# The second feed-forward product by seven block products instead of eight, with the splits of its tokens in another order

## Chip, cores and metric

One core of a Trainium2 chip. The metric is the device time of one execution in microseconds; the kernel before was run three times. The profiled execution is a run of its own.

## The reference, cut to what matters

Two transformer blocks in a row on 1024 tokens of width 1024, float32. The change touches the last lines of the second block, above all the second product:

```python
def second_block(x, c, ..., w_ff1, w_ff2):
    ...
    x = x + g1 * _hybrid_mixer(h, w_in[l], ...)
    h = _rms(x, norm2_w[l]) * (1 + sc2) + sh2
    x = x + g2 * (jnp.square(jax.nn.relu(h @ w_ff1[l])) @ w_ff2[l])
    return x
```

`w_ff1` is 1024 x 4096, `w_ff2` 4096 x 1024. Every product of the kernel keeps float32 accuracy with three matmuls: each operand is split in a high part (rounded to the type that TensorE multiplies) and a low part (the rest), and high x high, high x low and low x high are added in PSUM.

## The kernel before, in words

The kernel is one program of some fifteen stages, each written once per engine in fixed order, with semaphores between the engines. Weights lie in `wts` as slabs of 128 x 1024 numbers; activations lie transposed, features on the 128 partitions, tokens along the row, in two halves of 512 tokens.

**First product.** `mixer_out_stage` makes the first quarter of the 4096 hidden features in full (eight tiles x two halves). `ffn_stage` makes the other three quarters in 12 pairs of tiles. A pair is a 2 x 2 block product (two halves of the depth, two halves of the tokens, two tiles of features) done by the Winograd form of Strassen's scheme: seven products (`PRODUCTS`, line 2309) on four weight blocks and the sums S1 to S4 of them, against four token blocks and combinations of these that `mixer_out_stage` prepared. One product is 12 matmuls of 128 x 512 (four depth steps x three), a pair 84. GpSimd makes S1 to S4 and the seven low parts (lines 3660 to 3668), ScalarE the seven high parts (`pair_high`, line 3199) and a copy of the first product (line 3574), VectorE adds up the results out of six banks (`add`, line 3591), takes the square of the positive part (`square`, line 3599), and ScalarE's queue stores the four result blocks of 256 KB to `fd` in HBM (`store`, line 3552). SyncE's queue loads a pair's weights, three transfers of 1 MB together (lines 3691 to 3695), released by a product of the pair two before.

**Second product.** It is a plain product. The 4096 hidden features are taken in eight eighths of four tiles. For each eighth SyncE loads its tokens from `fd` in one transfer of 2 MB (`f_load`, line 3702), ScalarE makes four high parts of 1024 numbers a row (`eighth_high`, line 3563), VectorE four low parts (`eighth_low`, line 3604). Weights come as 512 KB for two output tiles through a ring of three (`ring_load`, line 3710); GpSimd casts them and makes the low parts (lines 3676 to 3679). TensorE makes, for each eighth, eight output tiles x two token halves, 12 matmuls each, in two banks by turns:

```python
for e in range(EIGHTHS):
    for f in range(KT):
        ...
        for c in range(2):
            pe.wait_ge(s_x2, 2 * i + c + 1)
            for j in range(KH):
                ...
```

VectorE multiplies each result by the gate and adds it to `x2` in SBUF (line 3644, one update for 12 matmuls); behind the last eighth SyncE stores each output tile of 512 KB (line 3739). In the last pair of the first product the two parts overlap: the first ring and token loads, the first eighth's splits on ScalarE (line 3581) and VectorE (lines 3621 and 3626), and the load of `x2`.

**Around it.** `gated_out_stage` closes each branch of the mixer; with `opens` it clears semaphores that later stages take again (lines 2282 to 2284, `k.again`). `leaves` marks the branch of the pooled features, its last use.

## Time and profile before

| | us |
|---|---|
| median of three runs (3139.1 to 3140.5) | 3140.2 |
| the profiled execution | 3137.1 |
| its span, from the first to the last instruction | 3135.3 |
| TensorE matmul busy | 3064.3 (98%) |
| VectorE busy | 1685.8 (54%) |
| GpSimd busy | 1444.7 (46%) |
| ScalarE busy | 987.1 (31%) |

The mean granted clock of TensorE is 0.996 of full speed. Busy time is the time in which an engine has an instruction under way. Matmuls of TensorE are pipelined and their recorded times overlap, so its count of instructions and the distance of their starts say more than the busy time. The span is 1.8 us shorter than the execution.

### The profile page before, as it was taken

Reading aid. Unit: us, or ns where it says so; the run is one execution under the profiler, and the core shown is the slowest. Engines: PE = TensorE matmul, PEld = TensorE weight load, DVE = VectorE, ACT = ScalarE, POOL = GpSimd, SP = SyncE. Lnnn points to the kernel's source line nnn. Section 1 sums busy time; section 2 is a strip of 40 time slices with the busy share of each in tenths; the row PEclk is TensorE's granted clock in tenths of the full one; section 3 lists DMA queues with packets and bytes.
Section 4 is the critical chain, followed back from the end, with each engine's and each line's share of the span. In section 5 each row is a group of like instructions: output and inputs, shape, how many; then the busy total and the mean of one; then the engine's idle time right before and its main releaser. Section 6 shows DMA issues by size and latency. Waiting matters only on the chain.

```text
span 3135.3 us, 39395 instructions
## 1 busy us (share of the span) xinstructions
PE 3064.3 (98%) x15012; PEld 2511.6 (80%) x15012; DVE 1685.8 (54%) x2636; ACT 987.1 (31%) x1520; POOL 1444.7 (46%) x1180
## 2 busy tenths in 40 slices
PE   8999999999999999999999999999999999999999
PEld 5777888887877777778788888888788878878887
DVE  5874666666444786655644343465624554444443
ACT  4445444454312532500433332431211232210000
POOL 3442211211356522223877777545336687743332
PEclk9999999999999999999999999999999999999999
DMA  4321100110144321255122222272124433342222
GB/s 143 101 77 41 34 28 27 34 34 27 48 134 148 95 82 45 70 167 204 49 78 70 65 64 83 81 221 71 49 88 161 144 118 116 116 178 101 101 102 87
DMA packets 119661, 288.84 MB, mean 92 GB/s; under 512 B 9904, under 2 KB 36144, under 8 KB 118080
## 3 DMA queue, kind: packets, MB, share of 16 engines
q1 hardware_dynamic: 75984, 219.25, 21.8%
q10 hardware_dynamic: 43504, 67.19, 6.2%
q8 instruction: 120, 1.97, 0.3%
q14 instruction: 53, 0.43, 0.0%
HBM read 239.05 MB, written 47.35 MB: 91 GB/s over the span
## 4 chain that ended last, share of the span: by engine, by line
PE 90%; DVE 6%; ACT 1%; issue 1%; DMA 1%; DVEq 0%; POOL 0%; ACTq 0%; SPq 0%; PEldq 0%; PEld 0%; POOLq 0%
PE proj_bank L236 13%; PE proj_bank L238 13%; PE proj_bank L237 13%; PE proj_bank L2492 4%; PE proj_bank L2494 4%; PE proj_bank L2493 4%; PE proj_bank L3544 4%; PE proj_bank L3546 4%; PE proj_bank L3545 4%; PE aux_banks L236 2%; PE aux_banks L238 2%; PE aux_banks L237 2%; PE aux_banks L3531 2%; PE aux_banks L3532 2%; PE aux_banks L3530 2%; PE aux_banks L795 2%
## 5 line engine op out<-in xcount | busy, mean ns | idle before, releaser
L253 POOL CAST slab_hi<-slab_raw 128x1024 fp32r<-128x1024 f32 x188 | 204.7, 1089 | 1250.6 <-PE proj_bank L238 723.0
L236 PE MATMUL proj_bank<-h_hi,slab_hi 128*128 128x512 f32 x1728 | 688.2, 398 | 10.2 <-ACT y L638 2.8
L238 PE MATMUL proj_bank<-h_hi,slab_lo 128*128 128x512 f32 x1728 | 675.3, 391 | 0.0
L237 PE MATMUL proj_bank<-h_lo,slab_hi 128*128 128x512 f32 x1728 | 674.7, 390 | 0.0
L257 POOL TENSOR_TENSOR slab_lo<-slab_raw,slab_hi 128x512 fp32r<-128x512 f32 x376 | 540.8, 1459 | 15.0
L236 PEld LDWEIGHTS proj_bank<-h_hi,slab_hi 128*128 128x128 f32 x1728 | 325.6, 188 | 89.1 <-issue 16.1
L238 PEld LDWEIGHTS proj_bank<-h_hi,slab_lo 128*128 128x128 f32 x1728 | 325.4, 188 | 69.5
L237 PEld LDWEIGHTS proj_bank<-h_lo,slab_hi 128*128 128x128 f32 x1728 | 325.9, 189 | 66.8 <-issue 2.2
L2818 DVE TENSOR_TENSOR pair_results<-proj_bank,pair_results 128x512 f32<-128x512 f32 x147 | 99.6, 690 | 213.9 <-PE proj_bank L2494 213.9
L3644 DVE SCALAR_TENSOR_TENSOR x_back<-proj_bank,mod,x_back 128x512 f32<-128x512 f32 x128 | 96.0, 750 | 212.5 <-PE proj_bank L3546 212.5
L3544 PE MATMUL proj_bank<-ffn_hi,ff_hi 128*128 128x512 f32 x512 | 200.1, 391 | 2.9 <-DVE ffn_lo L3606 2.9
L3545 PE MATMUL proj_bank<-ffn_lo,ff_hi 128*128 128x512 f32 x512 | 199.8, 390 | 0.0
L3546 PE MATMUL proj_bank<-ffn_hi,ff_lo 128*128 128x512 f32 x512 | 199.7, 390 | 0.0
L2982 POOL TENSOR_TENSOR pair_lo<-pair_sums,pair_hi 128x512 fp32r<-128x512 f32 x147 | 189.8, 1291 | 11.8
L3676 POOL CAST ff_hi<-ff_raw 128x1024 fp32r<-128x1024 f32 x32 | 33.3, 1040 | 225.3 <-DMA ff_raw<-wts 225.3
L2492 PE MATMUL proj_bank<-h_hi,pair_hi 128*128 128x512 f32 x336 | 133.9, 398 | 0.4 <-issue 0.4
L2494 PE MATMUL proj_bank<-h_hi,pair_lo 128*128 128x512 f32 x336 | 131.1, 390 | 0.0
L2493 PE MATMUL proj_bank<-h_lo,pair_hi 128*128 128x512 f32 x336 | 130.9, 390 | 0.0
L952 ACT ACTIVATE att_p<-aux_banks,small 128x256 f32<-128x256 f32 (+7 forms) x128 | 94.6, 741 | 113.1 <-DVE small L1059 95.4
L2980 POOL CAST pair_hi<-pair_sums 128x512 fp32r<-128x512 f32 x147 | 91.9, 625 | 76.8 <-PE proj_bank L2494 74.4
L3544 PEld LDWEIGHTS proj_bank<-ffn_hi,ff_hi 128*128 128x128 f32 x512 | 96.5, 188 | 23.2 <-DVE ffn_lo L3606 3.3
L3568 ACT ACTIVATE ffn_hi<-ffn_raw 128x1024 fp32r<-128x1024 f32 x32 | 31.2, 1047 | 263.3 <-DMA ffn_raw<-ffn_made 263.3
(486 smaller groups left out, 6412.5 us busy)
## 6 DMA issues: line engine op xcount, KB each, us to landing
slab_raw<-wts SPq DMA_DIRECT2D x190, 512.0 KB, 3.6
ffn_made<-ffn_made ACTq DMA_DIRECT2D x64, 256.0 KB, 2.4
ff_raw<-wts SPq DMA_DIRECT2D x32, 512.0 KB, 3.7
ffn_raw<-ffn_made SPq DMA_DIRECT2D x8, 2048.0 KB, 9.6
ada_w<-ada_w SPq DMA_DIRECT2D x40, 384.0 KB, 3.1
pair_sums<-wts SPq DMA_DIRECT2D x21, 512.0 KB, 3.7
ada_w_early<-ada_w SPq DMA_DIRECT2D x24, 384.0 KB, 3.5
ssd_decay_rows<-decay_sums ACTq DMA_DIRECT2D x16, 512.0 KB, 3.7
```

What stands on the lines that cost most here:

```text
L236: pe.matmul(bank, whi[:, slot, wk, :], hi[:, xk, cols], start=first and a == 0, stop=False)
L237: pe.matmul(bank, whi[:, slot, wk, :], lo[:, xk, cols], start=False, stop=False)
L238: mm = pe.matmul(bank, wlo[:, slot, wk, :], hi[:, xk, cols], start=False, stop=last and a == len(ks) - 1)
L253: pool.tensor_copy(whi[:, to], k.raw[:, slot]).then_inc(k.s_hi, 1)
L257: ins = pool.tensor_tensor(wlo[:, to, part], k.raw[:, slot, part], whi[:, to, part].bitcast(F32), ALU.subtract)
L2492: pe.matmul(bank(pr, i), dp.hi(i)[:, j, :], hi, start=j == 0, stop=False)
L2493: pe.matmul(bank(pr, i), dp.hi(i)[:, j, :], lo, start=False, stop=False)
L2494: mm = pe.matmul(bank(pr, i), dp.lo(pr, i)[:, j, :], hi, start=False, stop=j == KH - 1)
L2982: pool.tensor_tensor(dp.lo(pr, i), dp.sum(pr, i), dp.hi(i).bitcast(F32), ALU.subtract).then_inc(dp.s_split, 1)
L3544: pe.matmul(k.bank[c][:], ring_hi[d % RING][:, half, j, :], hi, start=j == 0, stop=False)
L3545: pe.matmul(k.bank[c][:], ring_hi[d % RING][:, half, j, :], lo, start=False, stop=False)
L3546: mm = pe.matmul(k.bank[c][:], ring_lo[d % RING][:, half, j, :], hi, start=False, stop=j == KH - 1)
```

## The change

The second product is done by the same seven-product scheme. A pair is now one eighth of the depth (two blocks of two tiles), four output tiles (two blocks of two) and both token halves: 16 pairs. The order of the products is `SECOND`. Each product is two halves `s` of six matmuls with an update each; U2 and U3 of the scheme are not formed by VectorE: S2, S3 and A22 go on adding in the bank that A11 began, S4 in the bank of S1, and the running value is added to the quadrant of the output that needs it. The token blocks T1 to T4 are formed by VectorE when the first product's blocks are made (`combined_first`, `combined_second`), for the first quarter by loading its blocks back during pairs 1 to 4 (`early`), and are stored to `fd` beside B11, B21 and B22; so an eighth now has seven blocks of 512 KB, each loaded, split and waited for by itself. The weights are in another order in `wts` and go through the first product's buffers, S1 to S4 and splits (the loops over pairs run over 28 instead of 12). `a21` moves to where the constants lay. 18 semaphores of the dilated stage are cleared at the start of the pool branch's output stage for use again.

```diff
+        for s in k.spent if opens or leaves else ():
+            dve.sem_clear(s)
...
+SECOND = (A11, A12, S2, S1, S3, S4, A22)
...
+    SLOT = {B11: 0, B22: 1, B21: 2}
+    second_bank = lambda d, i, s: (k.bank[s][:] if d % 2 == 0 else k.aux[:, 4 + s, :]) if SECOND[i] in (A11, S2, S3, A22) \
+        else k.aux[:, (0 if SECOND[i] == A12 else 2) + s, :]
...
+    def bank_free(d, i, s):
...
+        if a in (S2, S3, S4, A22):
+            return s_acc, reads(d, at[{S2: A11, S3: S2, A22: S3, S4: S1}[a]], s)
...
-        for e in range(EIGHTHS):
-            for f in range(KT):
...
+        for d in range(SECOND_PAIRS):
+            p, e = FF_PAIRS + d, d // 2
+            for i, a in enumerate(SECOND):
+                pe.wait_ge(k.s_split, N_WHOLE + N_PROD * p + i + 1)
+                if d % 2 == 0:
+                    pe.wait_ge(s_flo, N_PROD * e + i + 1)
+                for s in range(2):
+                    free = bank_free(d, i, s)
+                    if free is not None:
+                        pe.wait_ge(*free)
+                    to = second_bank(d, i, s)
+                    for j in range(2):
...
                     mm.then_inc(k.s_proj, 1)
...
+        def store_combined(p):
+            for which, (b, at) in enumerate(((T1, 3), (T2, 1), (T3, 0), (T4, 2))):
+                act.wait_ge(s_t, 4 * p + which + 1)
+                act.dma_start(block_of(p, b), n.made[:, at]).then_inc(k.s_x[at], 16)
...
             act.activation(n.p1, bank(p, 0), ACT.Copy).then_inc(n.s_tensor, 1)
             if p:
-                store(p - 1, 3)
-            if p < LAST:
-                for i in range(N_PROD):
-                    pair_high(k, act, n, p + 1, i)
+                store_combined(p - 1)
+            for i in range(N_PROD):
+                pair_high(k, act, n, p + 1, i)
             if p == LAST:
-                eighth_high(0)
+                token_high(0, 0)
+                token_high(0, 1)
...
+        def combined_first(p):
...
+            dve.tensor_tensor(b12, b12, b11, ALU.subtract).then_inc(s_t, 1)
...
+            dve.tensor_tensor(b22, b22, b12, ALU.subtract).then_inc(s_t, 1)
...
+        def token_low(e, t):
+            dve.wait_ge(s_fhi, N_PROD * e + t + 1)
+            dve.tensor_tensor(f_lo[e % 2][t][:], f_raw[e % 2][t][:], f_hi[e % 2][t][:].bitcast(F32), ALU.subtract).then_inc(s_flo, 1)
+
+        def accumulate(d, i):
...
+            for s in range(2):
...
+                dve.scalar_tensor_tensor(xt, second_bank(d, i, s), k.mod[:, 40 + f:41 + f], xt, ALU.mult, ALU.add).then_inc(s_acc, 1)
...
+        for d in range(SECOND_PAIRS):
+            for i in range(N_PROD):
+                accumulate(d, i)
+                low = lows(d, i)
+                if low is not None and low[0] < EIGHTHS:
+                    token_low(*low)
+                if d == 0 and i == 5:
+                    combined_first(LAST)
+                if d == 1 and i == 0:
+                    combined_second(LAST)
...
-        for p in range(FF_PAIRS):
+        for p in range(ALL_PAIRS):
...
-                sp.wait_ge(k.s_proj, product_done(p - 2, 5))
+                sp.wait_ge(k.s_proj, product_done(p - 2, 5 if p - 2 < FF_PAIRS else N_PROD - 1))
...
+            if FF_PAIRS + 1 < p < ALL_PAIRS - 1 and (p - FF_PAIRS) % 2 == 1:
+                token_load((p - FF_PAIRS + 1) // 2, range(N_PROD))
```

VectorE at the end of the last pair of the first product, before (L3597 is `add`, L3602 `square`, L3606 a low part of the tokens, L3644 an update):

```order
L3597 TENSOR_TENSOR ffn_made<-aux_banks,ff_u_20690 128x512
L3602 SCALAR_TENSOR_TENSOR ffn_made<-ffn_made 128x512
L3606 TENSOR_TENSOR ffn_lo_22118<-ffn_raw_22116,ffn_hi_22120 128x1024 x2
L3597 TENSOR_TENSOR ffn_made<-aux_banks,ff_p_20688 128x512
L3602 SCALAR_TENSOR_TENSOR ffn_made<-ffn_made 128x512
L3606 TENSOR_TENSOR ffn_lo_22118<-ffn_raw_22116,ffn_hi_22120 128x1024
L3597 TENSOR_TENSOR ffn_made<-aux_banks,ff_u_20689 128x512
L3602 SCALAR_TENSOR_TENSOR ffn_made<-ffn_made 128x512
L3606 TENSOR_TENSOR ffn_lo_22118<-ffn_raw_22116,ffn_hi_22120 128x1024
L3644 SCALAR_TENSOR_TENSOR x_back<-proj_bank,mod,x_back 128x512 x6
```

The same place with the change (L3673 is `add`, L3678 `square`, L3711 a low part, L3724 an update):

```order
L3711 TENSOR_TENSOR ffn_lo_1_22155<-ffn_raw_1_22141,ffn_hi_1_22127 128x1024
L3673 TENSOR_TENSOR ffn_made<-aux_banks,ff_u_20708 128x512
L3678 SCALAR_TENSOR_TENSOR ffn_made<-ffn_made 128x512
L3673 TENSOR_TENSOR ffn_made<-aux_banks,ff_p_20706 128x512
L3678 SCALAR_TENSOR_TENSOR ffn_made<-ffn_made 128x512
L3711 TENSOR_TENSOR ffn_lo_2_22156<-ffn_raw_2_22142,ffn_hi_2_22128 128x1024
L3673 TENSOR_TENSOR ffn_made<-aux_banks,ff_u_20707 128x512
L3678 SCALAR_TENSOR_TENSOR ffn_made<-ffn_made 128x512
L3724 SCALAR_TENSOR_TENSOR x_back<-proj_bank,mod,x_back 128x512 x2
L3711 TENSOR_TENSOR ffn_lo_3_22157<-ffn_raw_3_22143,ffn_hi_3_22129 128x1024
L3724 SCALAR_TENSOR_TENSOR x_back<-aux_banks,mod,x_back 128x512 x2
L3711 TENSOR_TENSOR ffn_lo_4_22158<-ffn_raw_4_22144,ffn_hi_4_22130 128x1024
```

Before, all four low parts of the first eighth stand ahead of the first update; now three stand ahead and four stand between the updates, one behind each product's two.

ScalarE in the last pair of the first product, before (L3574 is the copy of the first product, L3557 a store, L3568 a high part of the tokens):

```order
L3574 ACTIVATE ff_p_20688<-aux_banks 128x512
L3557 DMA ffn_made<-ffn_made 128x512
L3568 ACTIVATE ffn_hi_22120<-ffn_raw_22116 128x1024 x4
L3557 DMA ffn_made<-ffn_made 128x512 x4
L3568 ACTIVATE ffn_hi_22121<-ffn_raw_22117 128x1024 x4
```

and with the change (L3636 is the copy, L3617 a store of a combined block, L3227 a high part of weights, L3626 one of tokens, L3612 a store of a block):

```order
L3636 ACTIVATE ff_p_20706<-aux_banks 128x512
L3617 DMA ffn_made<-ffn_made 128x512 x4
L3227 ACTIVATE ff_pair_hi_20715<-ff_pair_sums_20711 128x512 x7
L3626 ACTIVATE ffn_hi_0_22126<-ffn_raw_0_22140 128x1024
L3626 ACTIVATE ffn_hi_1_22127<-ffn_raw_1_22141 128x1024
L3612 DMA ffn_made<-ffn_made 128x512 x2
L3626 ACTIVATE ffn_hi_2_22128<-ffn_raw_2_22142 128x1024
L3612 DMA ffn_made<-ffn_made 128x512
L3626 ACTIVATE ffn_hi_3_22129<-ffn_raw_3_22143 128x1024
L3626 ACTIVATE ffn_hi_4_22130<-ffn_raw_4_22144 128x1024
```

The four stores of combined blocks and the seven high parts of the next pair's weights now stand ahead of the tokens' first high part.

## Rows read from the trace of the kernel before

**Rows 1.** The page, shares of the chain that ended last, by engine.
```profile
PE 90%; DVE 6%; ACT 1%; issue 1%; DMA 1%; DVEq 0%; POOL 0%; ACTq 0%; SPq 0%; PEldq 0%; PEld 0%; POOLq 0%
```

**Rows 2.** Source view of line 3544: count, durations in ns (min/median/max), first and last start.
```profile
L3544 PE MATMUL proj_bank<-ffn_hi,ff_hi x512: 389/389/792, 2778.4 to 3130.6; 128*128 128x512 f32 x171
```

**Rows 3.** Timeline of VectorE, end: start, us, operation, idle before and releaser.
```profile
3128.80 0.75 DVE L3644 SCALAR_TENSOR_TENSOR x_back<-proj_bank,mod,x_back 128x512 f32<-128x512 f32 x1 [1.97 <-PE proj_bank L3546]
3131.52 0.75 DVE L3644 SCALAR_TENSOR_TENSOR x_back<-proj_bank,mod,x_back 128x512 f32<-128x512 f32 x1 [1.97 <-PE proj_bank L3546]
```

**Rows 4.** Waits of TensorE from 2530 on: us in total, times, longest.
```profile
PE proj_bank L3544 <- DVE ffn_lo L3606: 2.9, 1, 2.9
PE aux_banks L3530 <- DVE tokens_combined_lo L3443: 2.9, 1, 2.9
```

**Rows 5.** Timeline of TensorE behind the wait.
```profile
2784.93 0.63 PE L3544 MATMUL proj_bank<-ffn_hi,ff_hi 128*128 128x512 f32 x1
2785.36 0.63 PE L3545 MATMUL proj_bank<-ffn_lo,ff_hi 128*128 128x512 f32 x1
```

**Rows 6.** Windows: length, engines' busy time and instructions, clock, DMA share, GB/s.
```profile
2550.00:2552.00 2.00, 0.00 (x0) 0.00 (x0) 1.34 (x3) 1.08 (x2) 1.64 (x2) 1.00 0.19 71
2680.00:2699.00 19.00, 19.00 (x85) 15.76 (x84) 9.10 (x11) 4.58 (x8) 15.18 (x12) 1.00 0.33 111
2759.00:2778.20 19.20, 19.20 (x87) 15.89 (x86) 9.65 (x14) 4.51 (x5) 7.11 (x6) 1.00 0.95 369
2783.00:2785.00 2.00, 1.51 (x4) 1.22 (x5) 0.43 (x1) 0.00 (x0) 1.57 (x1) 0.63 0.99 421
```
The five busy times are those of TensorE's matmuls, its weight loads, VectorE, ScalarE and GpSimd.

**Rows 7.** Timeline of SyncE's queue, first loads of two pairs of the first product.
```profile
2661.61 0.33 SPq L3691 DMA_DIRECT2D ff_pair_sums<-wts  x1
...
2680.65 0.33 SPq L3691 DMA_DIRECT2D ff_pair_sums<-wts  x1
```

**Rows 8.** Source views of six lines.
```profile
L3644 DVE SCALAR_TENSOR_TENSOR x_back<-proj_bank,mod,x_back x128: 736/751/752, 2785.3 to 3131.5; 128x512 f32<-128x512 f32 x128
L3606 DVE TENSOR_TENSOR ffn_lo<-ffn_raw,ffn_hi x32: 1215/1217/2331, 2774.5 to 3077.8; 128x1024 fp32r<-128x1024 f32 x32
L3655 POOL TENSOR_TENSOR ff_pair_lo<-ff_pair_sums,ff_pair_hi x72: 1261/1298/1772, 2545.3 to 2755.0; 128x512 fp32r<-128x512 f32 x72
L3210 ACT ACTIVATE ff_pair_hi<-ff_pair_sums x72: 613/622/635, 2544.5 to 2748.5; 128x512 fp32r<-128x512 f32 x72
L3568 ACT ACTIVATE ffn_hi<-ffn_raw x32: 1038/1044/1064, 2772.0 to 3056.4; 128x1024 fp32r<-128x1024 f32 x32
L3602 DVE SCALAR_TENSOR_TENSOR ffn_made<-ffn_made x48: 682/1052/1820, 2562.2 to 2779.9; 128x512 f32<-128x512 f32 x48
```

**Rows 9.** Timeline of GpSimd between two pairs of the first product.
```profile
2681.03 1.30 POOL L3655 TENSOR_TENSOR ff_pair_lo<-ff_pair_sums,ff_pair_hi_late 128x512 fp32r<-128x512 f32 x1
2685.91 1.29 POOL L3660 TENSOR_TENSOR ff_pair_sums<-ff_a,ff_pair_sums 128x512 f32<-128x512 f32 x1 [3.59 <-DMA ff_a<-wts]
```

**Rows 10.** Timelines of GpSimd and VectorE where low parts meet, second product.
```profile
2842.47 2.54 POOL L3679 TENSOR_TENSOR ff_lo<-ff_raw,ff_hi 128x512 fp32r<-128x512 f32 x2
...
2843.87 2.22 DVE L3606 TENSOR_TENSOR ffn_lo<-ffn_raw,ffn_hi 128x1024 fp32r<-128x1024 f32 x1
...
2810.00 3.60 POOL L3679 TENSOR_TENSOR ff_lo<-ff_raw,ff_hi 128x512 fp32r<-128x512 f32 x2
...
2811.23 1.22 DVE L3606 TENSOR_TENSOR ffn_lo<-ffn_raw,ffn_hi 128x1024 fp32r<-128x1024 f32 x1
```

**Rows 11.** Source view of the clears; timeline of VectorE in the pool branch's output.
```profile
L2284 DVEq EVENT_SEMAPHORE_RANGE_CLEAR  x31: 54/54/54, 1341.5 to 1344.4; - x31
...
2283.43 0.69 DVE L2279 TENSOR_TENSOR pool_gate<-pool_gate,aux_banks 128x512 f32<-128x512 f32 x1 [13.97 <-PE aux_banks L238]
```

**Rows 12.** DMA issues from 2500 on: count, KB each, median us to landing.
```profile
ffn_made<-ffn_made ACTq DMA_DIRECT2D x58, 256.0 KB, 2.2
...
outT<-x_back SPq DMA_DIRECT2D x8, 512.0 KB, 2.6
```

More of the change, by code:

```diff
@@ L2297, in _ @@
         end(k, dve)
-    if opens:
+    if opens or leaves:
         k.cleared, k.spent = k.cleared + k.spent, []
@@ L3160, in pool_mix_stage, with product_order, made_block @@
     k.stage += 1
+SECOND = (A11, A12, S2, S1, S3, S4, A22)
+B11, B21, T2, T1, T3, B22, T4, B12 = range(8)
 WHOLE_DONE = 2 * N_WHOLE
 PAIRS_DONE = WHOLE_DONE + N_PROD * FF_PAIRS
+SECOND_PAIRS = 2 * EIGHTHS
+ALL_PAIRS = FF_PAIRS + SECOND_PAIRS
+def product_order(p):
+    return PRODUCTS if p < FF_PAIRS else SECOND
 def product_done(p, i):
-    return WHOLE_DONE + N_PROD * p + i + 1
+    if p < FF_PAIRS:
+        return WHOLE_DONE + N_PROD * p + i + 1
+    return PAIRS_DONE + 2 * (N_PROD * (p - FF_PAIRS) + i + 1)
+def made_block(row, c):
+    return ((B11, B12), (B21, B22))[row][c]
 def ffn_place(k):
@@ L3500, in ffn_stage @@
+    spare = [k.at(f"early_{b}", k.H + 32 * b, [P, KT, T])[:, 0:KH, HALF:T] for b in range(2)]
+    s_fl = [[k.again(f"ffn_loaded_{b}_{t}") for t in range(N_PROD)] for b in range(2)]
     s_fhi, s_flo = k.again("ffn_high"), k.again("ffn_low")
+    s_t, s_early = k.again("ffn_combined"), k.again("ffn_early_combined")
+    s_early_in, s_early_out = ([k.again(f"ffn_early_{name}_{b}") for b in range(2)] for name in ("loaded", "stored"))
     s_moved = n.s_x2_moved
-    s_x2, s_out = k.sem("x2_added"), k.sem("out_written")
+    s_acc, s_out = k.again("x2_added"), k.sem("out_written")
@@ L3506, in ffn_stage, with reads @@
     cols_of = lambda c: slice(c * HALF, (c + 1) * HALF)
     squared = 2 * KT
+    SLOT = {B11: 0, B22: 1, B21: 2}
+    second_bank = lambda d, i, s: (k.bank[s][:] if d % 2 == 0 else k.aux[:, 4 + s, :]) if SECOND[i] in (A11, S2, S3, A22) \
+        else k.aux[:, (0 if SECOND[i] == A12 else 2) + s, :]
+    QUADRANT = {A11: (0, 0), A12: (0, 0), S2: (0, 1), S1: (1, 1), S3: (1, 1), S4: (0, 1), A22: (1, 0)}
+    def reads(d, i, s):
+        return 2 * (N_PROD * d + i) + s + 1
+    def bank_free(d, i, s):
+        a = SECOND[i]
+        at = {x: m for m, x in enumerate(SECOND)}
+        if a in (S2, S3, S4, A22):
+            return s_acc, reads(d, at[{S2: A11, S3: S2, A22: S3, S4: S1}[a]], s)
+        if a == A11:
+            return (s_acc, reads(d - 2, at[A22], s)) if d >= 2 else (n.s_added, N_PROD * FF_PAIRS) if d else None
+        if d == 0:
+            return n.s_added, N_PROD * LAST + READ[(1 if a == A12 else 3) + s]
+        return s_acc, reads(d - 1, at[{A12: A12, S1: S4}[a]], s)
@@ L3575, in _ @@
             if p:
-                store(p - 1, 3)
-            if p < LAST:
-                for i in range(N_PROD):
-                    pair_high(k, act, n, p + 1, i)
+                store_combined(p - 1)
+            for i in range(N_PROD):
+                pair_high(k, act, n, p + 1, i)
             if p == LAST:
-                eighth_high(0)
+                token_high(0, 0)
+                token_high(0, 1)
             for which in range(3):
                 store(p, which)
-        store(LAST, 3)
-        for e in range(1, EIGHTHS):
-            eighth_high(e)
+                if p == LAST and which == 1:
+                    token_high(0, 2)
+            if 1 <= p <= EARLY:
+                store_early(p - 1)
+        for t in range(3, N_PROD):
+            token_high(0, t)
+        for d in range(SECOND_PAIRS):
+            p, e = FF_PAIRS + d, d // 2
+            if d % 2 and d > 1 and e + 1 < EIGHTHS:
+                for t in HIGHS[1]:
+                    token_high(e + 1, t)
+            for i in range(N_PROD if p + 1 < ALL_PAIRS else 0):
+                pair_high(k, act, n, p + 1, i)
+            if e + 1 < EIGHTHS and (d == 1 or d % 2 == 0):
+                for t in HIGHS[d % 2]:
+                    token_high(e + 1, t)
+            if d == 0:
+                store_combined(LAST)
         end(k, act)
@@ L3737, in _ @@
-        for f in range(KT):
-            sp.wait_ge(s_x2, 2 + 2 * KT * (EIGHTHS - 1) + 2 * f + 2)
-            sp.dma_start(out[:, f], x2[:, f]).then_inc(s_out, 16)
-        sp.wait_ge(s_out, 16 * KT)
+            if p == 1:
+                early_load(0)
+                early_load(1)
+            if p in (3, 4):
+                early_load(p - 1)
+            if p == FF_PAIRS + 1:
+                token_load(1, range(3))
+                sp.wait_ge(k.s_proj, product_done(LAST, N_PROD - 1))
+                x2_load(1)
+                token_load(1, range(3, 5))
@@ new lines, in _ @@
+            if p == FF_PAIRS + 2:
+                for at in range(4):
+                    sp.wait_ge(k.s_x[at], n.stored + 16 * (4 + (FF_PAIRS if at == 3 else 2 * FF_PAIRS)))
+                token_load(1, range(5, N_PROD))
+            if FF_PAIRS + 1 < p < ALL_PAIRS - 1 and (p - FF_PAIRS) % 2 == 1:
+                token_load((p - FF_PAIRS + 1) // 2, range(N_PROD))
+        for m in range(2):
+            d = SECOND_PAIRS - 2 + m
+            for row, c, i in ((0, 0, 1), (1, 1, 4), (0, 1, 5), (1, 0, 6)):
+                for s in range(2):
+                    f = 4 * m + 2 * s + row
+                    sp.wait_ge(s_acc, reads(d, i, s))
+                    sp.dma_start(out[:, f, cols_of(c)], x2[:, f, cols_of(c)]).then_inc(s_out, 16)
```

226 lines of the change are left out of this document (116 added, 110 removed).

## The prediction

> **What bounds the kernel now.** I read the page first: TensorE is busy for 98% of the span (the table above) and carries 90% of the chain that ended last [rows 1], so time leaves this kernel only where TensorE does fewer matmuls or idles less. Then the source view of the second product: its matmuls start at 2778.4 [rows 2], and the last one releases VectorE at 3131.5 [rows 3], 353.1 us for 1536 matmuls. A matmul is recorded with 389 ns, but they overlap. The price of one is the pitch: VectorE's last two updates are 2.72 us apart for 12 matmuls [rows 3], 0.2267 us each. 1536 of them are 348.2 us, so 4.9 us are lost. The waits and the timeline of TensorE say where: one wait of 2.9 us for a low part of the tokens at the start [rows 4], behind which matmuls run at a pitch of 0.43 us instead of 0.227 [rows 5] while the granted clock is 0.63 [rows 6], near the lower of the two levels (1.2 against 2.4 GHz). That leaves 2.0 us for the clock. Nothing else stalls.
>
> **The matmuls.** Seven products for eight: 16 pairs of 84, 1344 instead of 1536. 192 x 0.2267 = **43.5 us less**. The pitch should hold: the pairs of the first product, which have the same operands' shapes, take 19.04 us for 84 (SyncE's next loads, released by TensorE, start 19.04 us apart [rows 7]), again 0.2267.
>
> **Banks.** The group between two waits shrinks from 12 matmuls to 6. A sum is continued in a bank only after VectorE has read it; between lies one whole product and the other half, 3 x 1.36 = 4.1 us from the end of a half to its bank's next use. One update is 0.75 us [rows 8], so VectorE may be 3 us late before TensorE waits. Price taken: nothing in the steady part. If VectorE is later than that, see the rivals. The first-product pairs move to another bank with each of the seven products, and their granted clock stays 1.00 [rows 6]. The Trainium skill (TensorE: Matmul & The Clock Gate, "A second HAM failure mode: psum-queue depth-cycling") says that small idle times between groups that cycle through banks can make the clock oscillate; by that rule the gain would be given back in part or wholly, by the row nothing is. I go by the row.
>
> **VectorE, steady part.** In two pairs (38.1 us): 28 updates x 0.75 = 21.0, and seven low parts at 1.22 to 2.33 [rows 8], 8.5 to 16.3. Sum 29.5 to 37.3, so it fits even with every low part at its longest. The long ones come from meeting GpSimd: one low part takes 2.22 beside an undelayed GpSimd pair of operations (2.54), another takes 1.22 while GpSimd's two grow to 3.60 [rows 10]. About 1.05 us is paid for each meeting, by one or the other. The worst place is three neighbouring products (A22 and the two beside it) with a low part behind each: at 2.2 each VectorE comes 3.4 us late to A12, whose bank is not continued, and 2.1 to 2.5 us late to the banks that are (each product brings 2.72 us of time for 1.5 of updates and 2.2 of a low part). Under 3, so no wait.
>
> **GpSimd, steady part.** Eleven operations of 1.30 [rows 8] per pair are 14.3 us; the pairs of the first product, which do the same, show 15.18 busy of 19.0 [rows 6]. The 3.5 low parts of VectorE add at most 3.7, 18.0 of 19.04. Its start: SyncE now issues a pair's weights when TensorE leaves the pair two before (one product later than in the first product). From issue to GpSimd's first sum is 5.3 us (2680.65 to 2685.91 [rows 7, 9]), so the first low part is there at 5.3 + 4 x 1.3 = 10.5 of 19.04 and the last at 23.3 at worst, before the next start at 24.3. Hidden, with 8 us to spare at the point where TensorE waits.
>
> **ScalarE, queues.** Two pairs cost ScalarE 14 x 0.62 + 7 x 1.04 = 16.0 of 38.1 [rows 8]. The new loads are 7 blocks of 512 KB per two pairs beside 2 MB of weights: 5.8 MB in 38.1 us, 152 GB/s, while the stretch before the second product sustains 369 GB/s [rows 6]. On SyncE's queue the blocks stand behind the weights of the same pair and need some 10 us at that rate, so they are gone before the next weights at 19.04. Nothing.
>
> **First product.** Each pair gets four subtractions on VectorE, pairs 1 to 4 four more. The nearest row is the square, also 512 columns from SBUF: 0.68 to 1.82, median 1.05 [rows 8]. VectorE's 9.1 us per pair [rows 6] become 13.3, and 17.5 in pairs 1 to 4, of 19.04; it falls behind by about a microsecond, and six banks forgive 10. ScalarE now sits in front of T1 to T4's stores before it makes the next high parts: GpSimd's first low part moves from 6.4 to about 9 us after the pair starts, and its 3.59 us of idle time [rows 9] covers that. Nothing; if the cover were gone, the second product's weights would be late by the rest. The 18 semaphore clears at the start of the pool branch's output stage are 54 ns each at some 0.1 us pitch, in front of 13.97 us of waiting [rows 11]. Nothing.
>
> **The boundary.** Times from the start of the last first-product pair, which TensorE leaves at 19.04. ScalarE stores T1 to T4 and makes seven high parts, so the tokens' first high part comes at 11.9. With VectorE's SBUF operations at their contended values (squares 1.05, low parts 1.8) the line is: low part 0 at 13.7, two sums 15.0, square 16.1, low part 1 at 17.9, sum, square, sum, square 21.3, low part 2 at 23.1, sum and square 24.9, update of A11 at 25.6. TensorE wants that bank at 24.5: it waits 1.2. Low part 3, A12's update, low part 4 and S2's first update are done at 32.0 against 31.1, then S4's and A22's banks are each 0.5 late. Together 3.2 us in four small waits. With the uncontended values (0.69 and 1.22) there is none. I take 2 us, since GpSimd is busy until about 20 and then waits for the next weights, and 1 us for the clock (0 or 2.0: of two gaps of 2.9 us [rows 4] one kept the clock at 1.00 [rows 6], the other not). So 3 us lost for 4.9, **1.9 less**; ends 0 and 5.2.
>
> **The end.** The last update is the same; what follows stores 256 KB instead of 512: 2.2 for 2.6 us to landing [rows 12], **0.4 less**.
>
> Sum: 43.5 + 1.9 + 0.4 = 45.8 us. The profiled execution took 3137.1 us (its span 3135.3 and 1.8 around it), so 3091.3; the median of the runs shown is 3.1 us above it. I forecast against that median: **3094.4 us**. With the ends of the boundary (0 and 5.2 lost) it is 3091 to 3097. A difference under 0.2%, 6 us, is no difference here.
>
> **Rivals.**
> *VectorE or GpSimd too slow in the steady part.* For: 37.3 of 38.1 at worst leaves no room for semaphores between instructions. Against: back to back, VectorE's instructions show no such gap, and the median low part took 1.22 [rows 8]. If each pair loses 0.5 to 1.5 us, 8 to 24 come back: 3102 to 3118. Chance 0.13.
> *A longer boundary.* The blocks of tokens 2 to 6 are issued behind 3 MB; high part 2 is needed at 21. If they land 5 us later, or the waits each bring down the clock (four times 2.0), 5 to 10 us more: 3099 to 3104. Chance 0.11.
> *Half the saving does not appear.* The 224 new half groups each open with a wait; at 0.1 us each 22 us come back, 3117. Against: behind a group of 12 the next one starts with no idle time [rows 4]. Chance 0.03.
> *Slower: TensorE waits at one continued bank in every pair and loses its clock behind it.* Price as at the one stall of before: 2.9 + 2.0 = 4.9 us, 16 times, 78 us; less 45.8 that is 3173. It decides from 45.8 / 16 = 2.9 us per pair on. It needs VectorE 5.9 us late at a bank; against it stands the room reckoned above. This is the way the skill's rule would take (TensorE: Matmul & The Clock Gate, the section named above). Chance 0.03.
>
> **How the numbers follow.** Forecast 0.70, rivals 0.13, 0.11, 0.03, 0.03. The range runs 3088 (3091 less the 3 us by which the runs differ, the profiled one included), through the longer boundary and into the first rival as far as 3110, which leaves out about 0.13 above (the slower part of the first rival and the last two) and 0.03 below. All cases but the last are faster by more than 6 us: faster 0.96, within 0.2% 0.01, slower 0.03.
>
> **What would show it.** Right: 1344 matmuls of the second product in about 308 us with a pitch of 0.2267; TensorE's waits there under 4 us and all in the first pair; VectorE's update about 0.75 us and its low parts near 1.9 on the mean; GpSimd some 16 of 19 us busy. Wrong: waits of TensorE on VectorE's updates or GpSimd's low parts in the later pairs, a granted clock under 1.00 after 2830, or first-product pairs longer than 19.04.

## The result and the profile after

The kernel takes **3096.85 us** (median of four runs; 3093.67 to 3099.39) after 3139.77 (median of four): a ratio of 0.9863, 95% interval 0.9846 to 0.9880. The forecast was 3094.4, range 3088 to 3110. The profiled execution took 3095.93 us (forecast 3091.3), its span 3093.9: 41.4 us less than before instead of 45.8. The chain that ended last, by engine, on the page (against [rows 1]):

```profile
PE 89%; DVE 7%; ACT 1%; issue 1%; DMA 1%; ACTq 0%; POOL 0%; DVEq 0%; SPq 0%; PEldq 0%; PEld 0%; POOLq 0%
```

Source views of the second product's first matmul of three (one of its three groups of banks; against [rows 2]), of VectorE's update and low part (against [rows 8]) and of its second subtraction; at the end, VectorE's last update in its timeline (against [rows 3]):

```profile
L3596 PE MATMUL proj_bank<-ffn_hi,ff_pair_hi x128: 389/389/765, 2779.1 to 3070.8; 128*128 128x512 f32 x128
...
L3724 DVE SCALAR_TENSOR_TENSOR x_back<-aux_banks,mod,x_back x160: 733/746/753, 2790.0 to 3090.7; 128x512 f32<-128x512 f32 x160
L3711 DVE TENSOR_TENSOR ffn_lo<-ffn_raw,ffn_hi x56: 1205/1644/2340, 2775.1 to 3056.7; 128x1024 fp32r<-128x1024 f32 x56
L3687 DVE TENSOR_TENSOR ffn_made<-ffn_made x12: 692/1594/1597, 2573.7 to 2804.8; 128x512 f32<-128x512 f32 x12
...
3090.70 0.75 DVE L3724 SCALAR_TENSOR_TENSOR x_back<-aux_banks,mod,x_back 128x512 f32<-128x512 f32 x1 [0.61 <-PE aux_banks L3598]
```

The second product runs from 2779.12 to the end of its last matmul's pitch at 3090.51: 311.4 us for 1344 matmuls, which are 304.7 at 0.2267. So 6.7 us are lost in it, where 3 were forecast (4.9 before). Waits of TensorE from 2540 on (against [rows 4]), and its timeline behind the first of them (against [rows 5]):

```profile
PE proj_bank L3596 <- DVE x_back L3724: 3.4, 1, 3.4
PE aux_banks L3579 <- DVE tokens_combined_lo L3460: 2.9, 1, 2.9
PE aux_banks L3579 <- POOL ff_pair_lo L3774: 1.7, 1, 1.7
...
2784.58 0.39 PE L3598 MATMUL aux_banks<-ffn_hi,ff_pair_lo 128*128 128x512 f32 x1
2788.42 0.77 PE L3596 MATMUL proj_bank<-ffn_hi,ff_pair_hi 128*128 128x512 f32 x1 [3.45 <-DVE x_back L3724]
2788.98 0.63 PE L3597 MATMUL proj_bank<-ffn_lo,ff_pair_hi 128*128 128x512 f32 x1
2789.41 0.63 PE L3598 MATMUL proj_bank<-ffn_hi,ff_pair_lo 128*128 128x512 f32 x1
...
2795.36 0.39 PE L3596 MATMUL aux_banks<-ffn_hi,ff_pair_hi 128*128 128x512 f32 x1
```

The matmul after 2784.58 is due 0.23 later and comes at 2788.42: 3.6 us. From there to 2795.36 lie 18 matmuls in 6.9 us instead of 4.1: 2.9 us for the clock, which the windows show at its lower level. 3.6 + 2.9 is all but 0.2 of the 6.7. Windows (columns as in [rows 6]), and below them one of 19 us in the first product, behind pairs 1 to 4:

```profile
2787.00:2789.00 2.00, 0.58 (x2) 0.52 (x3) 2.00 (x4) 2.00 (x3) 1.42 (x2) 0.62 1.03 413
2789.00:2791.00 2.00, 2.00 (x6) 1.61 (x5) 2.00 (x3) 1.23 (x3) 2.00 (x1) 0.50 1.09 451
2900.00:3000.00 100.00, 100.00 (x443) 82.81 (x442) 79.94 (x92) 40.40 (x56) 82.69 (x58) 1.00 0.48 174
...
2680.00:2699.00 19.00, 19.00 (x85) 15.73 (x85) 18.59 (x18) 5.75 (x10) 18.69 (x13) 1.00 0.46 153
```

The wait is for A11's bank. The timelines of VectorE and ScalarE show what led to it:

```profile
2767.41 1.78 DVE L3696 TENSOR_TENSOR ffn_made<-ffn_made 128x512 f32<-128x512 f32 x1
...
2775.14 1.54 DVE L3711 TENSOR_TENSOR ffn_lo<-ffn_raw,ffn_hi 128x1024 fp32r<-128x1024 f32 x1 [4.62 <-ACT ffn_hi L3626]
...
2787.53 1.40 DVE L3724 SCALAR_TENSOR_TENSOR x_back<-proj_bank,mod,x_back 128x512 f32<-128x512 f32 x2
...
2764.12 5.43 ACTq L3617 DMA_DIRECT2D ffn_made<-ffn_made  x4
2769.64 2.72 ACT L3227 ACTIVATE ff_pair_hi<-ff_pair_sums 128x512 fp32r<-128x512 f32 x5 [6.05 <-DVE ffn_made L3696]
2773.00 1.15 ACT L3227 ACTIVATE ff_pair_hi<-ff_pair_sums 128x512 fp32r<-128x512 f32 x2 [0.64 <-POOL ff_pair_sums L3785]
2774.06 1.99 ACT L3626 ACTIVATE ffn_hi<-ffn_raw 128x1024 fp32r<-128x1024 f32 x2
```

ScalarE's queue issues the stores of T1 to T4 until T4 is made; then ScalarE makes the seven high parts of the next pair's weights and only then the tokens' first one. VectorE stands idle for 4.62 us and updates A11 at 2787.53, 2.7 us after TensorE wanted the bank. That was my theory when the experiments began (theory A below); the rivals were token blocks that land late, and a steady part that loses the time. In the profiles of after and e1 nothing at the boundary has a token block as its releaser.

### The profile page after: what moved, and what is told of

It is laid out like the page before. It is cut to its first block, busy times and chain, and to the rows that moved or that the text cites. A ratio compares the mean times of both kernels' runs of the same rounds, so it can differ in the third digit from the quotient of the medians.

```text
span 3093.9 us, 39758 instructions
## 1 busy us (share of the span) xinstructions
PE 3024.1 (98%) x14820; PEld 2477.4 (80%) x14820; DVE 1893.6 (61%) x2820; ACT 1073.9 (35%) x1656; POOL 1618.0 (52%) x1260
## 4 chain that ended last, share of the span: by engine, by line
PE 89%; DVE 7%; ACT 1%; issue 1%; DMA 1%; ACTq 0%; POOL 0%; DVEq 0%; SPq 0%; PEldq 0%; PEld 0%; POOLq 0%
PE proj_bank L236 13%; PE proj_bank L238 13%; PE proj_bank L237 13%; PE proj_bank L2493 4%; PE proj_bank L2495 4%; PE proj_bank L2494 4%; PE aux_banks L236 3%; PE aux_banks L238 2%; PE aux_banks L237 2%; PE aux_banks L3596 2%; PE aux_banks L3597 2%; PE aux_banks L3598 2%; PE aux_banks L3579 2%; PE aux_banks L3581 2%; PE aux_banks L3580 2%; PE aux_banks L795 2%
## 5 line engine op out<-in xcount | busy, mean ns | idle before, releaser
L3774 POOL TENSOR_TENSOR ff_pair_lo<-ff_pair_sums,ff_pair_hi 128x512 fp32r<-128x512 f32 x168 | 264.2, 1596 | 20.9 <-ACT ff_pair_hi L3227 17.1
L3227 ACT ACTIVATE ff_pair_hi<-ff_pair_sums 128x512 fp32r<-128x512 f32 x168 | 96.8, 623 | 230.6 <-DMA ff_a<-wts 100.1
L3724 DVE SCALAR_TENSOR_TENSOR x_back<-aux_banks,mod,x_back 128x512 f32<-128x512 f32 x160 | 115.8, 744 | 38.9 <-PE aux_banks L3598 38.6
L3598 PE MATMUL aux_banks<-ffn_hi,ff_pair_lo 128*128 128x512 f32 x320 | 124.5, 389 | 0.0
L1128 DVE COPY att_w_turned<-aux_banks 128x512 f32<-128x512 f32 (+2 forms) x96 | 52.9, 551 | 94.5 <-PE aux_banks L802 94.4
L2493 PE MATMUL proj_bank<-tokens_hi,pair_hi 128*128 128x512 f32 x252 | 101.4, 402 | 0.6 <-DVE tokens_lo L2814 0.6
L237 PE MATMUL proj_bank<-y_lo,slab_hi 128*128 128x512 f32 x256 | 101.0, 395 | 0.0
```

What stands on the lines that cost most here:

```text
L237: pe.matmul(bank, whi[:, slot, wk, :], lo[:, xk, cols], start=False, stop=False)
L2493: pe.matmul(bank(pr, i), dp.hi(i)[:, j, :], hi, start=j == 0, stop=False)
L3598: mm = pe.matmul(to, n.lo(p, a)[:, 2 * s + j, :], hi, start=False, stop=j == 1, skip_group_check=True)
L3724: dve.scalar_tensor_tensor(xt, second_bank(d, i, s), k.mod[:, 40 + f:41 + f], xt, ALU.mult, ALU.add).then_inc(s_acc, 1)
L3774: pool.tensor_tensor(n.lo(p, a), own(a), n.hi(p, a).bitcast(F32), ALU.subtract).then_inc(k.s_split, 1)
```

## The experiments

The four or more runs of one kernel lie 2 to 7 us apart, so the table also gives, from one profile of each, the length of the first product (from its first matmul's start to the start of its last L3579, whose number is up to 3 higher where lines were added) and what the second loses (from there to the start of the last matmul, less 1346 x 0.2267: 1344 and the two that end the first product). The loss of e3 holds its 15 added matmuls, 3.4 us. "After" stands in the first row.

| kernel | median us | first product | second loses |
|---|---|---|---|
| after | 3096.85 | 231.1 | 6.7 |
| e1 unchanged | 3097.82 | 232.7 | 5.6 |
| e2 low part later | 3101.20 | 232.6 | 8.1 |
| e3 gap filled | 3098.61 | 233.9 | 5.8 |
| e4 subtractions narrow | 3094.45 | 232.7 | 2.4 |
| e5 x_back later | 3095.70 | 232.4 | 4.3 |
| e6 both later | 3095.94 | 232.5 | 3.7 |
| e7 token high parts first | 3095.75 | 234.0 | 5.0 |
| e8 load 2 x 7 | 3144.55 | 234.0 | 54.0 |
| e9 x_back split | 3094.01 | 233.9 | 2.2 |
| e10 the same, first gap filled | 3094.92 | 231.0 | 4.5 |
| e11 load 1 x 7 | 3114.37 | 231.1 | 21.0 |

The kernel before took 3140.19, 3139.44 and 3140.18 us beside e1 to e4, e5 to e8, and e9 to e11.

**e1, the kernel unchanged.** 

> The kernel after the change, unchanged, on the chip of the three kernels that follow: what they are compared with. All theories expect 3094 to 3099 us, a profile with one wait of TensorE on VectorE's update in the second product (3.4 us) and a granted clock of about 0.5 for some 6 us behind it. If the spread of several us between runs is this one event coming and going (the clock falls behind the gap in some executions and not in others), other executions differ by about 3.6 us; if it is something elsewhere, the second product takes 311.6 us here too.

The event is the same: waits for the update, 3.7 us in all, the clock at 0.52 behind, 5.6 lost. What makes this profile longer than that of after lies elsewhere: its first product is 1.6 us longer.

**e2, the low part later.**
```
             if p == LAST:
-                token_low(0, 0)
...
             square(1, at + 3)
             if p == LAST:
+                token_low(0, 0)
                 token_low(0, 1)
```


> The first low part of the tokens is taken by VectorE two squares later in the last pair of the first product, so VectorE does not stand idle for 4.6 us ahead of it, waiting for ScalarE's high part. Theory A (the four subtractions of that pair take 1.65 us each, ScalarE stores them before it makes the first high part, the low part waits for that, and the update of A11 comes 2.6 us late to TensorE; the clock falls behind this gap): the wait of 3.4 us goes or shrinks below 1, small waits of 0.3 to 1 us may take its place, the clock stays at 1.00, and the time falls by 3 to 7 us against the unchanged kernel. Rival B (the token blocks arrive late from DRAM, so that any order of VectorE waits): the gap stays within 0.5 us and so does the time. Rival C (the 7 us lost are not the gap's but lie in the steady part): no difference of over 1 us in the second product.

A miss: 8.1 us are lost instead of 5.6, the median is 3.4 us higher, and two waits of over 2 us stand for the one. VectorE stands idle ahead of its next sum, for another releaser (timeline of VectorE, and of TensorE):

```profile
2781.58 0.69 DVE L3673 TENSOR_TENSOR ffn_made<-aux_banks,ff_u 128x512 f32<-128x512 f32 x1 [6.37 <-DMA ffn_made<-ffn_made]
...
2786.92 0.47 PE L3596 MATMUL proj_bank<-ffn_hi,ff_pair_hi 128*128 128x512 f32 x1 [2.32 <-DVE ffn_lo L3711]
2794.87 0.47 PE L3596 MATMUL proj_bank<-ffn_hi,ff_pair_hi 128*128 128x512 f32 x1 [2.23 <-DVE x_back L3724]
```

The sum into slot 1 must wait until T2 is stored from it. The stores of T1 to T4 of this pair take up to 10.9 us to land, where the median of such stores from 2600 on is 2.0: 3 MB of loads were issued ahead of them (blocks 0 and 1, half of x_back). The stores are issued from 2768.81 on, the sum starts 12.8 later. In the profile of after the same distance is 2764.12 to 2776.79, 12.7: there the sum came straight behind the low part, so its wait could not be seen. Two chains ended within the same microsecond, and the wait names one; e5 and e6 test this.

**e3, the gap filled.**
```
+                if d == 0 and i == 2:
+                    pe.wait_ge(n.s_added, N_PROD * LAST + READ[3])
+                    for _ in range(15):
+                        pe.matmul(k.aux[:, 2, :], n.hi(p, A11)[:, 0, :], f_hi[0][0][:, 0], start=True, stop=True)
```


> The order is unchanged, but TensorE does 15 further matmuls (into a bank that is overwritten later) in the place where it waited 3.4 us. They add nothing to the output. 15 x 0.2267 = 3.4 us of work. Theory A (a gap of 3.4 us and a clock that falls because of it, 3.6 us more): the gap is gone, the clock stays at 1.00 and the second product is about 3.6 us shorter, less what later small waits give back (the low clock had hidden that VectorE was late at the next banks: up to 2 us). Rival (the clock falls for another reason, such as the half groups or the cycling banks at that place): it falls here too, and the time stays within 1 us.

Timelines of VectorE (first row) and TensorE, and a window:

```profile
2788.33 1.23 DVE L3715 TENSOR_TENSOR ffn_lo<-ffn_raw,ffn_hi 128x1024 fp32r<-128x1024 f32 x1 [0.17 <-ACT ffn_hi L3630]
...
2789.65 3.69 PE L3592 MATMUL aux_banks<-ffn_hi,ff_pair_hi 128*128 128x512 f32 x15 [1.42 <-issue]
2793.18 0.39 PE L3600 MATMUL proj_bank<-ffn_hi,ff_pair_hi 128*128 128x512 f32 x1
...
2791.00:2793.00 2.00, 2.00 (x11) 1.62 (x10) 2.00 (x3) 2.00 (x4) 1.92 (x2) 1.00 1.09 439
```

The clock stays at 1.00. One profile alone would not settle it, since a gap does not bring the clock down every time (last section); but in e4 and e9, where no wait of the second product is over 1 us, it stays up as well. So in after and e1 it fell because of the gap. The time does not improve, since the fill begins 1.4 us late. It stands behind TensorE's wait for the tokens' third low part, which ends at 2789.56 (first row); its own bank had been read long before. So the next product starts 11.3 us after the first product's last L3579, in e1 9.5 (2793.18 less 2781.92, 2791.61 less 2782.07). What the clock gave, some 2 us, the late fill took, so the run tells of the cause of the clock and nothing of the gain. It shows besides that the update was not the only thing late: with A11's update in time, TensorE would have waited 1.4 us here for the low part.

**e4, the subtractions on one column.** The edit: `[:, 0:1]` on every operand of the four; nearly all of T1 to T4 is left out.

> The four subtractions T1 to T4 of each pair of the first product are done on 1 column instead of 512, so nearly all of that arithmetic is left out; their order, waits and stores stay. They cost VectorE 6.7 us per pair in the kernel after. Theory A (hidden in the steady first product, on the path only in its last pair): pairs of the first product stay 19.04 us apart, the second product starts at the same time, but the high parts of the tokens come some 6 us earlier, the wait of 3.4 us goes and the clock stays up: 5 to 7 us less. Rival (the subtractions also cost the first product something, by meeting GpSimd): the second product starts earlier, by some 0.3 us per pair or more. Rival B (token blocks late): the first product as in theory A, but the gap stays.

The first product takes the same as in e1, 232.7 us: these 6.6 us per pair are hidden. The second loses 2.4 instead of 5.6, with waits of 0.96 and 0.49 us and the clock at 1.00. So the subtractions reach the end only through the boundary, as theory A says. Its size was a miss: 3.2 us by the profiles and 3.4 by the medians, where 5 to 7 were expected. The first low part starts 6.8 us before the second product (2777.09, 2783.91) instead of 4.0 in after, 2.8 us earlier and not some 6: ScalarE waits 2.3 us for TensorE ahead of the weights' high parts and 1.5 for GpSimd's sum S4 between them.

**e5, e6, e7: the second chain, then both.** e5 issues half of x_back behind the token blocks; e6 adds e2's edit; e7 is e5 with the tokens' first two high parts ahead of the pair's seven on ScalarE.
```
                 token_load(0, range(2))
-                x2_load(0)
                 sp.wait_ge(k.s_proj, product_done(LAST, 3))
                 token_load(0, range(2, 6))
+                x2_load(0)
...
             if p == LAST:
                 token_high(0, 0)
                 token_high(0, 1)
             for i in range(N_PROD):
                 pair_high(k, act, n, p + 1, i)
```


> What the earlier kernels left open: with the first low part taken later, VectorE stood idle just as long, for the landing of the store of T2 (10.9 us instead of 2.0), which frees the slot of its next sum. Theory A2: two chains end in the same microsecond (ScalarE's high part of the tokens behind the stores of T1 to T4, and the landing of T2's store behind 3 MB of loads), so that taking away one alone brings nothing. Here only the second goes: the 2 MB load of the first half of x_back is issued behind the token blocks 2 to 5 instead of ahead of them; the order of the instructions on VectorE and ScalarE is unchanged. A2: T2's store lands some 5 us earlier, but VectorE still waits about 4.6 us for ScalarE ahead of the low part, TensorE's wait stays within 1 us of 3.4, and the second product is no shorter. Rival (DMA alone is the cause): the wait goes, 3 to 6 us less. Rival (x_back now comes late to the first update): a new wait of TensorE on the update, slower by 2 to 6 us.

> Both chains are taken away: the 2 MB load behind the token blocks and the first low part behind the square. Theory A2: VectorE takes its two sums and the square (3 us) while ScalarE makes the high part, so A11's update comes about 3 us earlier than in the unchanged kernel; TensorE's wait falls from 3.4 to under 1 us in one place (small waits of up to 1 us elsewhere), the clock stays at 1.00, and the second product loses 1 to 3 us instead of 5.6 to 6.7: 3 to 5 us less. Rival (x_back late to the first update): TensorE waits there 2 us or more.

> Both chains are taken away in another manner: the 2 MB load is issued behind the token blocks, and ScalarE makes the tokens' first two high parts ahead of the seven high parts of the next pair's weights instead of behind them, so the low part can be taken 4 us earlier in VectorE's unchanged order. GpSimd gets its high parts 2 us later, of which it has 4.5 us to spare where it waits for the next weights. Theory A2: VectorE's idle time of 4.6 us shrinks to about 1, A11's update is 3 us or more earlier, TensorE's wait of 3.4 goes, clock 1.00, 3 to 5 us less. Rival (GpSimd has no room): TensorE waits for a low part of the weights in the first pair of the second product, time unchanged or longer.

VectorE's idle times in the three, in this order, two rows for e5 (the stores of T1 to T4 now land in 5.7 us at most):

```profile
2776.03 1.55 DVE L3711 TENSOR_TENSOR ffn_lo<-ffn_raw,ffn_hi 128x1024 fp32r<-128x1024 f32 x1 [4.63 <-ACT ffn_hi L3626]
2788.04 1.41 DVE L3724 SCALAR_TENSOR_TENSOR x_back<-proj_bank,mod,x_back 128x512 f32<-128x512 f32 x2 [0.56 <-DMA x_back<-x_kept]
```
```profile
2774.31 4.33 DVE L3711 TENSOR_TENSOR ffn_lo<-ffn_raw,ffn_hi 128x1024 fp32r<-128x1024 f32 x2 [1.40 <-ACT ffn_hi L3626]
```
```profile
2789.06 1.41 DVE L3724 SCALAR_TENSOR_TENSOR x_back<-proj_bank,mod,x_back 128x512 f32<-128x512 f32 x2 [3.92 <-DMA x_back<-x_kept]
```

e5: with one chain gone the other holds the low part for 4.63 us, as A2 said; the wait of TensorE is still 2.7, and 4.3 us are lost, 1.3 less than in e1, where A2 had expected no gain; x_back's load already holds the update for 0.56 us. e6: both gone, the wait is 1.9, not under 1, and it brings the clock down: a miss, though a smaller loss (3.7). From 2774.31 on VectorE works without a stop, with two low parts of 2.2 us each, so its own work is the limit. e7: VectorE comes to A11's update at 2785.14, before TensorE wants it, and then waits 3.92 us for the load that I had moved: a third chain, made by the experiment itself, and a second miss.

**e9, all three.** Half of x_back in two: the columns that A11 and A12 update first stay in front.
```
-                x2_load(0)
+                x2_load(0, cols_of(0), 0)
                 sp.wait_ge(k.s_proj, product_done(LAST, 3))
                 token_load(0, range(2, 6))
+                x2_load(0, cols_of(1), 1)
```
(with e7's order on ScalarE, and the update waiting for its own half)

> All three chains that end at A11's update are taken away. ScalarE makes the tokens' first two high parts ahead of the pair's; the 2 MB load of x_back is cut into its two halves of the columns: the one that A11's and A12's updates need (1 MB) stays ahead of the token blocks 2 to 5, the other goes behind them. Theory A3 (VectorE waits at the boundary for whichever is last of ScalarE's high part, T2's store and x_back, and behind these VectorE's own work is the limit): no wait of TensorE over 1 us in the second product, clock 1.00 there, 1 to 3 us lost in it instead of 5.6 to 6.7, the low parts of GpSimd still in time. Rival (the DMA engines, at 400 to 430 GB/s from 2774 to 2800, are the limit whatever the order): another load, a token block or the next weights, is late and the wait appears there; 4 us or more lost.

```profile
PE proj_bank L3596 <- DVE x_back L3724: 1.0, 2, 0.7
PE aux_banks L3596 <- DVE x_back L3724: 0.2, 1, 0.2
...
2787.00:2789.00 2.00, 2.00 (x10) 1.69 (x9) 2.00 (x2) 1.00 (x1) 0.37 (x1) 1.00 1.03 407
```

Three waits, 1.2 us together, no fall of the clock, 2.2 us lost, as expected. The DMA engines are as full as before (407 GB/s here, 413 in after at the same place), so what held VectorE was the order in which the transfers were issued and not their rate. The median is 3094.01, 2.8 us under that of after, and its ratio to before, 0.9854 (0.9837 to 0.9870), overlaps e1's, 0.9865 (0.9849 to 0.9882): that it is the faster kernel of the two is shown in the trace and not by the times.

**e10, the older gap.** Twelve matmuls into bank(0, 1) at p = 0, i = 1 of the first product, ahead of its wait for the combined tokens' low parts.

> The kernel before this one, and 12 further matmuls of TensorE (2.7 us, overwritten later) in the place of its wait of 2.9 us for the low part of the combined tokens in the first pair of the first product, which stands in the kernel before the change too. Seven of the profiles so far show the clock at about 0.50 for some 3 to 5 us behind that wait, those of before and of after do not; it is what the first product's length differs by (231.1 against 232.4 to 234.0 us). Theory (this gap's clock is a part of the 3 us by which the runs of one kernel differ): the first product takes 231.1 us or less, the clock stays at 1.00 behind it, and the runs are 1.5 to 3 us faster than the kernel before this one. Rival (the clock falls there for another reason): the same length as without the matmuls.

The first product takes 231.0 us instead of 233.9, with the clock at 1.00. One profile does not show that the filling did it: before, after and e11 have 231.1 and the clock at 1.00 without it. The second loses 4.5 us, since the clock falls again behind a wait of 2.4: the stores of T1 to T4 took up to 8.3 us to land instead of 6.1, and T2's held VectorE for 2.31. The runs were expected 1.5 to 3 us faster than e9's; the median is 0.9 higher, a miss. Why the stores were slower with the same queue order stays open.

**e8 and e11, load on VectorE in the steady part.**
```
+            for x in range(2 if e >= 2 else 0):
+                dve.wait_ge(s_early, 4 * EARLY + 2 * (N_PROD * (e - 2) + t) + x)
+                dve.tensor_tensor(extra, f_hi[e % 2][t][:, 0, :256].bitcast(F32), f_hi[e % 2][t][:, 1, :256].bitcast(F32), ALU.subtract).then_inc(s_early, 1)
```


> Load put on VectorE in the steady part of the second product: two further subtractions of 256 columns into a spare kilobyte ahead of each low part of the tokens, from the third eighth on (35 low parts, 70 instructions; they add nothing to the output). At 0.35 us each (a 512-column one takes 0.68 alone) that is 4.9 us per two pairs, at twice that, as beside GpSimd, 9.8; VectorE is busy 30.1 to 35.6 of 38.1 us there. Theory A (VectorE has 2.5 to 8 us of room per two pairs, and TensorE forgives it being up to 3 us late): time within 5 us of the unchanged kernel, waits of TensorE on updates under 3 us in total. Rival, the slower one of the prediction (every late bank costs a gap and the clock behind it, 4.9 us each): waits in most pairs, 20 to 80 us slower.

> As the load of two instructions for each low part, but one: 7 per two pairs at the 0.81 us that they were measured to take there, 5.7 us more on a VectorE that is busy 30.4 of 38.1 us on the mean. With two (11.4 us, 41.8 of 38.1) TensorE waited 38 us for updates and the kernel took 48 us longer. Theory A (what counts is whether VectorE's sum exceeds the 38.1 us of two pairs; the banks forgive an uneven order): 36.1 of 38.1 fits, time within 3 us of the unchanged kernel, no wait over 1 us after the first pair. Rival (single late banks cost a gap each before the sum is full): waits in several pairs, 5 to 25 us slower.

Waits of TensorE on updates (e8, then e11), and two of e11's nine places:

```profile
PE aux_banks L3597 <- DVE x_back L3728: 35.0, 18, 5.9
PE proj_bank L3597 <- DVE x_back L3728: 3.2, 2, 3.1
```
```profile
PE aux_banks L3597 <- DVE x_back L3728: 12.0, 9, 2.7
...
2979.40 0.47 PE L3597 MATMUL aux_banks<-ffn_hi,ff_pair_hi_late 128*128 128x512 f32 x1 [1.96 <-DVE x_back L3728]
...
3020.44 0.47 PE L3597 MATMUL aux_banks<-ffn_hi,ff_pair_hi_late 128*128 128x512 f32 x1 [1.96 <-DVE x_back L3728]
```

With 11.4 us more per two pairs (0.81 each on the mean, where I had expected 0.35 to 0.70) the whole gain is gone: some 48 us slower than after. With 7 x 0.88 = 6.2 us more it is 17.5 us slower than after by the medians and 15.0 by the profiled executions, although VectorE's sum still fits (busy 34.5 to 35.7 of 38 us in the windows). Theory A fell in both, the rivals hold: in e11, once in two pairs (2979.40, 3020.44, 41 us apart), TensorE waits 2.0 us for an update. In front of the first of them VectorE has no idle moment from 2961.2 on: three neighbouring products with a low part behind each, the place that the prediction had picked as the worst, and one more. So the steady part was right at no cost, but its room is set at the worst place, where the banks forgive some 3 us, and not by the 7.6 us that VectorE is idle in two pairs.

## Why the prediction held, and where it was off

- **Matmuls, 43.5 us: right.** The pitch is 0.2267 and nothing waits after the first pair; the window 2900 to 3000 shows TensorE full.
- **Banks and clock, nothing: right.** The clock is 1.00 from 2795 to the end. The rule of the Trainium skill (TensorE: Matmul & The Clock Gate, "A second HAM failure mode: psum-queue depth-cycling") did not come about: without idle times, changing banks cost no clock. The slower rival is real, and e8 is its picture. With 6.2 us more work per two pairs (e11) TensorE waited, but the clock fell in the second product only behind the two waits of 2.7 us; the price at which the rival eats the whole gain was reached with 11.4 (e8).
- **VectorE, 29.5 to 37.3 of 38.1: right**, 79.94 of 100 us is 30.5; its low parts are 1.73 on the mean, its updates 0.74. **GpSimd** up to 18.0 of 19.04: 82.69 of 100 is 15.7, but the window 2840 to 2878 has 36.94 of 38, 18.5 per pair, so its worst case was put too low. **ScalarE** 16.0: 15.4. Loads 152 GB/s: 153 in e9's steady windows.
- **First product, nothing: right in the result, wrong in the term, and by a small margin.** A subtraction was taken at the square's median, 1.05, and most take 1.59 to 1.78. The timelines of VectorE and TensorE in after (the first two rows are the same sum in pairs 2 and 3):

```profile
2599.37 0.68 DVE L3673 TENSOR_TENSOR ff_u<-aux_banks,ff_p 128x512 f32<-128x512 f32 x1
2620.12 0.68 DVE L3673 TENSOR_TENSOR ff_u<-aux_banks,ff_p 128x512 f32<-128x512 f32 x1
...
2648.47 0.67 DVE L3673 TENSOR_TENSOR ff_u<-aux_banks,ff_u 128x512 f32<-128x512 f32 x1
...
2645.84 0.39 PE L3579 MATMUL aux_banks<-h_hi,ff_pair_hi 128*128 128x512 f32 x1
```

A pair with eight subtractions takes VectorE 20.75 us without an idle moment, more than TensorE's 19.04, where 17.5 were forecast. So VectorE falls behind by 1.7 us with each of the four, where the forecast had about one in all, and the six banks absorb it. At the tightest place VectorE has read a bank at 2649.14 (third row), and TensorE, which begins pair 5 at 2645.84 (fourth row), needs that bank with the pair's third product, 2 x 2.72 us later, at 2651.28: an estimate of 2.1 us to spare. In the kernel before, the same reckoning leaves 12. VectorE works the backlog off by 2700 (18.59 of 19 us busy in the window from 2680, with four subtractions). That it cost nothing was in part luck: by this estimate a fifth pair with eight would have left 0.4 us.
- **The boundary, 3 us lost: mis-sized; 6.7.** This is the step that failed. The tokens' first high part was put at 11.9 us after the last pair's start and was there at 15.0 (2775.06, the pair starts at 2760.08): 2.4 us for four slower subtractions, which ScalarE's stores wait for; of the other 0.7, ScalarE's timeline shows 0.64 as its wait for GpSimd's sum S4 between the weights' high parts. The late start made one wait of 3.6 us out of the four small ones that were priced at 2 us together, and the clock cost 2.9 where 1 was taken and 2.0 was the end of the range. That T2's store lands over 10 us after its issue and ends in the same microsecond stood nowhere in the working, nor that half of x_back, moved behind the token blocks, lands only when A11's update is due (e5, e7): I had priced the queues at their total, "nothing".
- **The end, 0.4 less:** 3.2 us from the last update's start to the span's end instead of 3.8, 0.6. The second product starts 0.7 us later (2779.1 for 2778.4), with a first product of the same 231.1 us: the difference lies ahead of it and is within what runs differ by.
- Sum: 43.5 - 1.8 + 0.6 - 0.7 = 41.6, measured 41.4; forecast 45.8. The median came out 2.5 us above the forecast and inside its range; that is less than the runs of one kernel differ by.

## To carry to other kernels

Where a stage changes and every queue is full, price the landing of each transfer that frees or fills a buffer there by its place in the queue, not by the sum of bytes; and when a wait is removed, look for what ends within a microsecond of its releaser, for the profile names the last one only. An engine's idle share is not its room: the room is what the buffers forgive at the place with the most work in a row, and a small added load finds it. Where a few rounds of a loop hold more work than the others, add up how far the engine falls behind over all of them, and compare that with what the buffers hold. Take a duration from rows in which both engines meet, if they will meet.
